# Convolution sums in PSUM: banks reassigned and five taps moved in a fused two-block transformer kernel

## The reference

```python
def second_block(x, ...):
    xn = rmsnorm_2(h, g_mix)
    z = xn @ w_in + b_in                    # (512, 1536)
    a, gate, p = z[..., :512], z[..., 512:1024], z[..., 1024:]
    u = a * sigmoid(gate)
    v = causal_depthwise_conv(u, w_dw)      # 31 taps for each of 512 channels
    y_conv = silu(layernorm(v + b_dw))
    # p: 4 groups of 128 channels, trailing mean over 2, 4, 8, 16 tokens
    # less the token itself, a 128x128 map for each group, a scale for each channel
    y_pool = multiscale_pool_group(p, w_pool, s_pool)
    h = h + concat(y_conv, y_pool) @ w_out
    h = h + swiglu_2(rmsnorm_2(h, g_ffn), w_gate, w_up, w_down)
    return rmsnorm_2(h, g_final)
```

## Time and profile before

| | |
|---|---|
| time, median of 3 runs | 1940.22 us (1939.79 to 1940.90) |
| span of the profiled execution | 1940.7 us |
| TensorE (PE) busy | 1863.6 us, 96% |
| VectorE (DVE) busy | 893.9 us, 46% |
| ScalarE (ACT) busy | 660.9 us, 34% |
| GpSimd (POOL) busy | 848.8 us, 44% |

### The profile page before, as it was taken

How to read it: one execution, slowest core, us unless ns; L and a number is a source line. 1 busy time by engine, 2 the same in 40 slices (tenths; PEclk the granted TensorE clock), 3 DMA queues, 4 the chain that set the end, 5 groups by cost and what they waited for, 6 DMA issues and landing times.

```text
span 1940.7 us, 22811 instructions
## 1 busy us (share of the span) xinstructions
PE 1863.6 (96%) x8194; PEld 1456.3 (75%) x8194; DVE 893.9 (46%) x1254; ACT 660.9 (34%) x1003; POOL 848.8 (44%) x379
## 2 busy tenths in 40 slices
PE   7999999999999999999999999999967999999997
PEld 5888888778776566667878888888753778888886
DVE  4333330377776876446633333302799353333102
ACT  4332321353223444446333323211523343332212
POOL 4444444544444322323454444444664254444443
PEclk9999999999999999999999999999987999999998
DMA  4222222323332111111222222222210122222221
GB/s 170 97 97 97 97 98 94 118 81 104 112 99 83 60 55 39 36 42 55 101 84 98 97 97 97 97 95 95 87 55 33 58 84 97 97 97 97 98 97 54
DMA packets 48763, 167.38 MB, mean 86 GB/s; under 512 B 5816, under 2 KB 6328, under 8 KB 48576
## 3 DMA queue, kind: packets, MB, share of 16 engines
q1 hardware_dynamic: 45216, 160.27, 23.6%
q10 hardware_dynamic: 3488, 6.31, 1.0%
HBM read 161.82 MB, written 2.11 MB: 84 GB/s over the span
## 4 chain that ended last, share of the span: by engine, by line
PE 86%; DVE 10%; ACT 2%; issue 1%; DMA 1%; ACTq 0%; DVEq 0%; SPq 0%
PE bank L458 23%; PE bank L460 23%; PE bank L459 23%; PE bank L640 7%; PE bank L674 4%; DVE conv_out L1473 3%; PE bank L702 3%; DVE input_low L1163 1%; PE bank L687 1%; DVE head_root L1302 1%; PE bank L790 1%; DVE tile L1293 1%; PE bank L583 1%; DVE residual L1199 1%; DVE tile L1294 1%
## 5 line engine op out<-in xcount | busy, mean ns | idle before, releaser
L384 POOL TENSOR_TENSOR weights_low<-raw_weights,weights_high 128x1024 fp32r<-128x1024 f32 x296 | 732.1, 2473 | 1070.3 <-ACT weights_high L851 1070.1
L458 PE MATMUL bank<-input_high,weights_high 128*128 128x512 f32 x1488 | 594.3, 399 | 39.6 <-DVE input_low L1163 20.9
L851 ACT CAST weights_high<-raw_weights 128x1024 fp32r<-128x1024 f32 x296 | 311.2, 1051 | 923.7 <-PE bank L460 883.9
L459 PE MATMUL bank<-input_high,weights_low 128*128 128x512 f32 x1488 | 584.7, 393 | 0.0
L460 PE MATMUL bank<-input_low,weights_high 128*128 128x512 f32 x1488 | 584.3, 393 | 0.0
L458 PEld LDWEIGHTS bank<-input_high,weights_high 128*128 128x128 f32 x1488 | 282.7, 190 | 113.2 <-issue 32.5
L460 PEld LDWEIGHTS bank<-input_low,weights_high 128*128 128x128 f32 x1488 | 282.5, 190 | 60.4
L459 PEld LDWEIGHTS bank<-input_high,weights_low 128*128 128x128 f32 x1488 | 282.9, 190 | 59.7 <-issue 2.6
L458 PE MATMUL bank<-hidden_high,weights_high 128*128 (+1 forms) x528 | 205.4, 389 | 0.0
L459 PE MATMUL bank<-hidden_high,weights_low 128*128 (+1 forms) x528 | 205.4, 389 | 0.0
L460 PE MATMUL bank<-hidden_low,weights_high 128*128 (+1 forms) x528 | 205.4, 389 | 0.0
(11 more groups left out here) (219 smaller groups left out, 1890.4 us busy)
## 6 DMA issues: line engine op xcount, KB each, us to landing
raw_weights<-weights SPq DMA_DIRECT2D x296, 512.0 KB, 3.3
tile<-tile ACTq DMA_DIRECT2D x36, 64.0 KB, 2.2
residual<-x_t SPq DMA_DIRECT2D x4, 512.0 KB, 8.5
tile<-forget_sums ACTq DMA_DIRECT2D x8, 256.0 KB, 3.2
out_t<-out_t SPq DMA_DIRECT2D x8, 256.0 KB, 2.1
mem_in<-mem_t ACTq DMA_DIRECT2D x1, 1024.0 KB, 6.0
causal_mask<-causal_mask SPq DMA_DIRECT2D x1, 256.0 KB, 7.7
positions_in<-positions SPq DMA_DIRECT2D x1, 256.0 KB, 9.4
```

What stands on the lines that cost most here:

```text
L384: pool.tensor_tensor(wl[:, u % SPL, :], raw[:, u % RAW, :], wh[:, u % SPL, :].bitcast(F32), ALU.subtract).then_inc(low_done, 1)
L458: pe.matmul(out, wh[:, u % SPL, w], rh, start=start, stop=False)
L459: pe.matmul(out, wl[:, u % SPL, w], rh, start=False, stop=False)
L851: act.copy(wh[:, u % SPL, :], raw[:, u % RAW, :]).then_inc(high_done, 1)
```

## The change

The running sums of chunks 1 and 2 move from SBUF (`conv_out`) to PSUM banks 6 and 7; the last tap of a chunk reads PSUM and writes `conv_out`. The input projection cycles over banks 0, 1 and 2, where it had 0, 1 and 7. The four pool maps share banks 4 and 5, so the third waits until ScalarE has copied the first out. The pool half takes its output chunks in another order: 2 to 5 for all four groups, then 6 and 7, whose banks must be free of the sums, then 0 and 1. Of chunk 0, VectorE now has taps 0 to 10 and GpSimd 20 taps (11 to 30), one in a step where it had two; the rest stays for the last step.

```diff
-POOL_TAPS = {0: range(6, TAPS)}
+POOL_TAPS = {0: range(11, TAPS)}
...
-POOL_STEP_TAPS = 2
+POOL_STEP_TAPS = 1
...
-POOL_HALF = [(k, m) for k in range(4, DK) for m in range(2, DK)] + [(k, m) for k in range(4, DK) for m in range(2)]
+POOL_HALF = [(k, m) for ms in ((2, 3, 4, 5), (6, 7), (0, 1)) for k in range(4, DK) for m in ms]
...
         proj = [bank[0], bank[1], bank[7]]
+        proj2, tap_sums, gathered, maps = bank[0:3], {1: bank[6], 2: bank[7]}, bank[0], bank[4:6]
...
-                project(U_IN2 + j, proj[j % 3][:, :], xh, xl, U_IN2 + j + 1)
+                project(U_IN2 + j, proj2[j % 3][:, :], xh, xl, U_IN2 + j + 1)
...
-                        pe.matmul(bank[2 + g][:, :], wpool[:, g, :], pooled[:, g, :], start=True, stop=True
+                        if g >= 2:
+                            pe.wait_ge(sem("pool_out"), g - 1)
+                        pe.matmul(maps[g % 2][:, :], wpool[:, g, :], pooled[:, g, :], start=True, stop=True
...
+                    if m in (6, 7) and k == 4:
+
+                        pe.wait_ge(sem("conv_done"), m - 5)
...
-                act.activation(ymix[:, 4 + g, :], bank[2 + g][:, :], ACT.Copy, scale=v("s_pool_2", g)
+                act.activation(ymix[:, 4 + g, :], maps[g % 2][:, :], ACT.Copy, scale=v("s_pool_2", g)
...
+                        total = tap_sums[c][:, :] if c in tap_sums else conv[:, c, :]
                         if k == 0:
-                            ins = dve.tensor_scalar(conv[:, c, :], src, w, v("b_dw_2", c), ALU.mult, ALU.add)
+                            ins = dve.tensor_scalar(total, src, w, v("b_dw_2", c), ALU.mult, ALU.add)
                         else:
-                            ins = dve.scalar_tensor_tensor(out=conv[:, c, :], in0=src, scalar=w, in1=conv[:, c, :],
-                                                           op0=ALU.mult, op1=ALU.add)
+                            ins = dve.scalar_tensor_tensor(out=conv[:, c, :] if k == TAPS - 1 else total, in0=src,
+                                                           scalar=w, in1=total, op0=ALU.mult, op1=ALU.add)
```

More of the change, by code:

```diff
@@ L764, in _ @@
             down("g2", "ffn2", U_DN2)
-            pair_start("mix2", U_IN2, proj[0][:, :], proj[1][:, :])
+            pair_start("mix2", U_IN2, proj2[0][:, :], proj2[1][:, :])
             for j in range(2, len(IN2_STEPS)):
@@ L789, in _ @@
                     pe.wait_ge(sem("in2_taken"), 10)
-                mm = pe.matmul(bank[0][:, :], diagonals[:, t, :], glu[:, c, k:k + S], start=(t == 0),
+                mm = pe.matmul(gathered[:, :], diagonals[:, t, :], glu[:, c, k:k + S], start=(t == 0),
                                stop=(t == len(taps) - 1))
@@ L1507, in _ @@
                 dve.wait_ge(unit_done, U_IN2 + j + 1)
-                dve.tensor_tensor(out, proj[j % 3][:, :], rstd[:, :], ALU.mult).then_inc(sem("in2_taken"), 1)
+                dve.tensor_tensor(out, proj2[j % 3][:, :], rstd[:, :], ALU.mult).then_inc(sem("in2_taken"), 1)
                 if kind == "s":
@@ L1537, in _ @@
                 dve.wait_ge(sem("taps_gathered"), 1)
-                dve.tensor_tensor(conv[:, c, :], conv[:, c, :], bank[0][:, :], ALU.add).then_inc(sem("conv_done"), 1)
+                dve.tensor_tensor(conv[:, c, :], conv[:, c, :], gathered[:, :], ALU.add).then_inc(sem("conv_done"), 1)
             for c in POOL_TAPS:
```

## The result

The changed kernel takes 1924.07 us (median of four runs, 1919.94 to 1927.19) against 1940.56 for the kernel before on the same chip; the ratio is 0.9914, 95% interval 0.9898 to 0.9931. It is faster by 0.9%. Forecast were 1921.4 us in a range of 1915 to 1930.

A forecast was written before the change was run, and what follows sets the result against it. PE bounds the kernel, waiting in the second block's projection and convolution for GpSimd's splits and VectorE's windows. The layer norm's first sum moves from 1513.46 to 1494.7, 18.8 us less: 1921.4 us, range 1915 to 1930.

The forecast's parts named there:

- The tap's price: VectorE's taps with sums in PSUM: 0.784 us each, as SBUF taps without contention; bounds 0.69 and 1.40.
- Rival A: PSUM taps have a longer pitch, each reading what the one before just wrote; at 0.90 us, 1926 us; chance 0.14.
- B: PSUM taps at the high bound of 1.40 us each: 12.4 us above the median, 1953 us; chance 0.05.
- D: PSUM taps faster still, at the low bound of 0.69 us: 1917.7 us; chance 0.09.
- Rival C: A tap with an SBUF first input and a pointer still waits for GpSimd: 1942 us; chance 0.06.
- The five extra SBUF taps: Chunk 0 taps moved to VectorE, in a step that had none: 6.8 us, the change's own cost.
- The gapped units: Four PE projection units held back by late VectorE takes: gaps of 1.0 to 1.4 us instead of up to 5.4.
- The eleven adds: GpSimd's chunk 0 adds left for the last step, 1.69 us each, from 1451.8, in one row of 17 to 19 us.
- the last bias: ScalarE's bias of the last pool chunk, queued behind its scaling for the 11th GpSimd add: at 1465.1, VectorE waiting 1.1 us.
- the third windows: VectorE's third pooled windows, worked beside GpSimd's adds: 6.25 us as before, VectorE through at 1464.0.
- The two map banks: PE's third map waits for ScalarE's copy of the first; costs nothing, since the fourth waits for windows until 1471.9.
- From the last maps to the sum: PE's stretch from the last maps to the layer norm's first sum: 22.7 us as before, sum at 1494.7.

The follow-up runs named there:

- run 11: Changed kernel with chunk 0 taps shared out as before; taps of chunks 1 and 2 read the first tap's result from PSUM and write SBUF: span 1912.1 us.
- run 10: Changed kernel with chunk 0 taps shared out as before; taps of chunks 1 and 2 read the first tap's result from SBUF and write PSUM: span 1939.0 us.
- run 5: Changed kernel with the four pool maps over three banks instead of two: 1921.70 us, stage 109.54 against 109.58.
- run 4: The changed kernel again with no edit, to see its spread: 1922.02 us, median of six runs.
- Run 2: Changed kernel with sums in PSUM but chunk 0 taps shared out as before (VectorE taps 0 to 5, two GpSimd adds a step): 1914.63 us.
- run 6: Changed kernel with two GpSimd adds a step and VectorE's eleven chunk 0 taps also summed in a third PSUM bank: 1913.50 us.
- run 3: Changed kernel with two GpSimd adds a step instead of one: 1919.72 us, stage 104.90.

## Why the prediction was right, step by step

To compare with the prediction's times, 1.24 us is added to those of the profile after, since its stage starts that much earlier.

- **The tap's price** was taken at 0.784 us from one to the next. Measured: 4.71 us for six, and 755 ns for one. Rival A, a dearer tap in PSUM, B, and D, a cheaper one, are out. The 62 cycles (an estimated 65 ns) that the Trainium skill, "VectorE: DVE Perf Modes", section on the TRN2 errata, has on top for a PSUM source don't show here: 755 and 747 ns stand against 742 for two SBUF operands. Rival C, that a tap with an SBUF first input still waits for GpSimd, is out by the same 755 ns and by run 11 (747). The Trainium skill, "SBUF — State Buffer", section "Who interferes with whom", has two SBUF inputs as what makes a VectorE instruction contend with a GpSimd one that reads SBUF. The trace agrees: in run 10 an output in PSUM doesn't help (1396 ns).
- **The five extra SBUF taps**: 6.8 forecast, 6.82 measured, and unit 3 taken until 1405.2 as forecast.
- **The gapped units**: forecast starts 1409.55, 1421.75, 1434.0 and 1440.9; measured 1409.55, 1421.96, 1434.31 and 1441.33. The last unit ends at 1446.9 (forecast 1446.4).
- **The eleven adds** begin at 1451.5 (forecast 1451.8) and take 16.79 us, 0.2 under the 17 to 19: I had each at 1.69, but beside PSUM taps an add needs only 1.29. So the last bias ends at 1463.6 instead of 1465.1. On the other side the third windows take 7.8 us, not 6.25: the last operation of the row of before was already behind the adds. And a split held up the second windows more than I gave them. VectorE is thus at the last windows at 1466.4 and doesn't wait for the bias at all, where I had 1465.1 after a wait of 1.1. The adds end at 1468.3, 2 us earlier than by my sum, so the last windows take 4.8 us and not 6.8, and end at 1471.2 (forecast 1471.9). The end fits because these errors cancel, and that is luck.
- **The two map banks** cost nothing, as said, and run 5 shows it. PE's idle ahead of the third map is 5.2 us where about 7 were forecast, since the bias comes earlier and PE's taps begin later.
- **From the last maps to the sum** 22.7 was forecast and 22.3 measured. The sum starts at 1493.7 (forecast 1494.7), so the stage gives 19.8 us instead of 18.8.
- **The median** is 2.7 us above the forecast although the stage is 1.0 better than it: the runs of the kernel scatter by 7 us, and in the profiles taken this comes from the clock in a stretch that neither the change nor the prediction touches (run 4).

What the prediction didn't see, though its terms contained it, is that the change is two changes of opposite sign. It priced the five taps (6.8 us) and the longer row of adds, but only inside one sum, and never asked what the kernel would be without them. Run 2 answers: 5.7 us faster still. My own figure for that, 9 us, was too large for the same reason as above, the windows beside GpSimd's adds.

## What to carry to other kernels

Beside a busy GpSimd, a VectorE operation with two SBUF tensor inputs pays some 0.9 us for an add and 2 us for a split that it meets (1.68 and 2.78 us against 0.74); a tap whose running sum is held in PSUM has only one SBUF input and stays at 0.755 us, and GpSimd's own operations shorten too. Once that is done, work moved off GpSimd helps only if it goes into PSUM as well (run 6) and costs if it stays in SBUF. Test the two parts of such a change apart, since the second relieves a contention that the first removes. A wait that is taken away in front of an engine that waits again later only moves; look at which operation it then stands before, and at what clock that one runs.

## What the runs showed of the hardware

- The first tap, a multiply and add of two scalars from SBUF, takes 0.81 us when it writes PSUM, and 0.55 when it writes SBUF while GpSimd is idle. But beside GpSimd's adds the SBUF one took 1.40, though it has a single SBUF tensor input, so a single SBUF input isn't enough in every operation to escape the wait. As one tap in 31 it hardly matters here. From the kernel before:

```profile
1402.06 1.40 DVE L1471 TENSOR_SCALAR conv_out<-glu_padded,vectors 128x512 f32<-128x512 f32 x1
```

- The layer norm's sums, eight records of a float32 matmul of 128x512, take 3.60 us without idle ahead, 5.40 after 2.21 us of idle, 6.33 after 4.16 and 6.78 after 4.60. The window over them has a granted clock of 1.00, 0.68, 0.58 and 0.54, thus between the 2.4 GHz level and, at the end, almost the 1.2 GHz one:

```profile
1490.65:1497.40 6.75, 6.75 (x9) 2.90 (x10) 0.00 (x0) 0.00 (x0) 0.00 (x0) 0.54 0.23 78
```

- The length of the idle alone doesn't decide: gaps of 0.9 to 1.3 us ahead of projection units, and the one of 2.09 us in run 3, cost the first matmul 0.08 us (0.47 instead of 0.39) and left the clock up. What else differs ahead of the sums wasn't tried and stays open.
